# Two projections of the second mixer by high and low parts with two raw weight tiles, and gather slots shared out anew

## The chip, the cores and the metric

The kernel is one program on one core of a Trainium2 chip. The metric is the device time of one execution in microseconds. All data are fp32.

## The reference, cut to what matters

Two transformer blocks run one after the other on 512 tokens of width 1024. Each has a mixer and then a feed-forward layer of experts: every token chooses 16 experts for each of 8 heads, 128 in all, and reads a row `u` and a row `v` of the expert table for each. The second block's mixer is what the change touches.

```python
h = rmsnorm(x, norm1_g)
z = h @ w_in                      # 1024 x 5896, split into nine parts
fq, fk, fv, ff, sq, sk, sv, mq, gl = jnp.split(z, splits, axis=-1)
...                               # three attentions on the parts
gates = jax.nn.sigmoid(gl + b_gate).reshape(B, S, 3, D)
merged = (gates[:, :, 0] * (o_fox @ w_fox_o) + gates[:, :, 1] * (o_swa @ w_swa_o)
          + gates[:, :, 2] * (o_mem @ w_mem_o))
x = x + merged @ w_out
x = x + peer_ffn_2(rmsnorm(x, norm2_g), ...)
# in peer_ffn_2, for each token: e = 128 chosen experts, g = their gates
act = gelu(u[e] @ h) * g
out = act @ v[e]
```

## The kernel before

Activations stand transposed, channels on the partitions and tokens along the row: `xT` and `hT` are 8 chunks of 128 channels by 512 tokens. From the first feed-forward layer on the kernel works on halves of 256 tokens.

**The gather.** The expert layers of both blocks are one stream of 1024 slots: 2 layers x 4 token tiles x 128 chosen experts. A slot reads for each of 128 tokens one row of 2048 fp32 (`u` and `v` side by side, 8 KB) by an indirect DMA that GpSimd issues (`Gather.pool`, L243). VectorE multiplies the `u` half with the token's activation and sums (L309), ScalarE takes the gelu for pairs of slots (L282), VectorE multiplies with the gate (L304), ScalarE makes a diagonal matrix of the weight (L289), and TensorE adds the weighted `v` half into PSUM with four fp32 matmuls (L263). There are 8 row buffers (`BUFS`); the DMA of a slot is issued when the slot 8 before it has been added.

**Beats.** The stream runs inside the other stages. Each stage is a block with one program per engine, and all engines leave it together. A stage is given a range of slots and spreads them evenly over its own steps: after its step i every engine runs its part of the slots of beat i (`Beats.at`). `shared_out` divides a range among the stages of a mixer in proportion to the lengths in `MIXER_LENGTHS`; the ranges are 266 to 508 for the first half of the second mixer and 522 to 764 for the second. `later` holds the slots beside the second tile's choice. A tile's gather can't begin before its choice is finished (`chosen`); what is left runs in `drain_stage`, with nothing beside it.

**The second mixer of one half**, in order: `n3` (norm), `p2` (23 chunks of 128 columns of `w_in_2`: queries, keys, values), `hn` (head norms), `vt` (turning the values), `foxa` (three attentions), `pg` (24 chunks: the gates), `mg2` (merge), `po2` (8 chunks), `n4`, then the query stage `c4` or `c6`, which computes the queries of the experts (16 chunks) and chooses them for its two token tiles. The length named "choose" covers the query chunks and the first tile's choice. The first block's query stage `c2` is the same code; its length "query" is 82 of 266, for 266 slots. Tiles are named by stage, with the half's digit left out: `p2h_ps`, `pgh_w`.

**`project_beside_stage`** (L609), used for `p2` and `pg`, has five weight tiles of 512 KB each (`WEIGHT_TILES`), the first being `first_tile`, loaded in the stage before. SP loads tile n when the product of chunk n - 5 is made. TensorE multiplies the landed fp32 tile with the fp32 activations: 8 products of 128x128 by 256, which the trace shows as 16 matmul instructions (L645). VectorE copies the result from PSUM (L656). ScalarE does nothing but the gather.

**`project_stage`** (L472), used for `p1` (512 tokens) and `poa` (256 tokens) in the first mixer, splits both factors into a high part of type float32r and the remainder: ScalarE copies the raw tile to `whi` (L521), VectorE subtracts to get `wlo` (L565), and the same for the activations once per stage (`hhi` L528, `hlo` L601). TensorE makes three products per 128x128 piece, high by high, high by low, low by high (L546 to L548), 24 matmul instructions per chunk. There are two each of `raw`, `whi` and `wlo`. SP loads raw tile n when `wlo` of n - 2 is made (L510), ScalarE copies when the tile has landed and the product of n - 2 is made. It already has a form that hosts beats (`hosting`), which no call uses.

## Time and profile before

| | us |
|---|---|
| median of 3 runs | 3988.92 (3985.97 to 3993.56) |
| the profiled execution | 3991.26 |
| its span, first to last instruction | 3989.4 |

| engine | busy us | share of the span |
|---|---|---|
| TensorE matmul | 3057.4 | 77% |
| VectorE | 2370.5 | 59% |
| GpSimd | 1152.4 | 29% |
| ScalarE | 915.4 | 23% |

The mean granted clock of TensorE is 0.830 of full speed. The gather's queue moves 1073.81 MB of the 1263.90 MB in all; the gather runs from about 810 us to the end. The second mixer of the first half begins at about 1575 us, that of the second half at about 2465; the last stretch, gather alone, begins at about 3436. Shares of busy time are averages over stages with different limits, so the stretches of single stages are what to read. A matmul's duration in the profile overlaps the next one's; the time that it takes is the distance between two starts.

### The profile page before, as it was taken

How to read it: one execution, taken by the hardware profiler on the slowest of the kernel's cores; microseconds unless marked ns; L12 is line 12 of the kernel's file. 1: busy time of each engine (PE TensorE's matmuls, PEld its weight loads, DVE VectorE, ACT ScalarE, POOL GpSimd, SP SyncE). 2: the span in 40 equal slices, each digit the busy share in tenths (PEclk: the TensorE clock that was granted, in tenths of full speed). 3: DMA queues.
4: the chain of work that ended last, by engine and by line, in shares of the span. 5: the costliest groups of instructions: out<-in, count | busy, mean ns of one | idle time of the engine just before them, and what ended most of it. 6: DMA issues, size and time to landing. Idle time of an engine off the chain costs nothing. (4 is left out here: it accounts for less than half of the span.)

```text
span 3989.4 us, 51160 instructions
## 1 busy us (share of the span) xinstructions
PE 3057.4 (77%) x18686; PEld 1577.7 (40%) x18686; DVE 2370.5 (59%) x6158; ACT 915.4 (23%) x2506; POOL 1152.4 (29%) x1029
## 2 busy tenths in 40 slices
PE   5975596756787765988899865979798876676666
PEld 4853395612354211633455522634465531111111
DVE  6557745476446677457545577457645578655554
ACT  2113232012111112136321111136412111111111
POOL 0000000043333444323323342323333334444442
PEclk8998698867798876977999986969999987766666
DMA  5510002289999999988999997977999999999998
GB/s 214 188 68 1 6 4 93 97 364 400 350 384 372 419 411 393 400 322 309 367 398 373 370 406 269 411 286 264 348 416 376 360 398 395 413 419 417 420 420 354
DMA packets 207064, 1263.90 MB, mean 317 GB/s; under 512 B 25748, under 2 KB 28948, under 8 KB 72356
## 3 DMA queue, kind: packets, MB, share of 16 engines
q0 software_dynamic: 147456, 1073.81, 67.3%
q1 hardware_dynamic: 59368, 186.95, 12.6%
q8 instruction: 143, 2.34, 0.2%
q14 instruction: 97, 0.79, 0.1%
HBM read 1256.17 MB, written 4.46 MB: 316 GB/s over the span
## 5 line engine op out<-in xcount | busy, mean ns | idle before, releaser
L243 POOL DMA_INDIRECT held_z<-in_experts,held_expert x512 | 579.0, 1131 | 1274.6 <-PE held_acc L263 907.6
L263 PE MATMUL held_acc<-held_z,held_diag 64*64 64x512 f32 x4096 | 697.6, 775 | 286.8 <-ACT held_diag L289 262.9
L263 PE MATMUL held_acc<-held_pair,held_diag 64*64 64x512 f32 x4096 | 688.9, 768 | 253.8 <-ACT held_diag L289 248.9
L243 POOL DMA_INDIRECT held_pair<-in_experts,held_expert x512 | 569.6, 1112 | 1047.6 <-PE held_acc L263 971.4
L309 DVE CUSTOM_DVE_ANT_0 held_z<-held_z,held_hrow 128x1024 f32<-128x1024 f32 x512 | 625.5, 1223 | 377.4 <-DMA held_z<-in_experts,held_expert 371.1
L309 DVE CUSTOM_DVE_ANT_0 held_pair<-held_pair,held_hrow 128x1024 f32<-128x1024 f32 x512 | 625.4, 1223 | 369.3 <-DMA held_pair<-in_experts,held_expert 360.7
L289 ACT ACTIVATE held_diag<-held_bands,held_weight 128x64 f32<-128x64 f32 x1024 | 347.7, 340 | 1467.7 <-DVE held_weight L304 1434.3
L263 PEld LDWEIGHTS held_acc<-held_z,held_diag 64*64 64x64 f32 x4096 | 135.2, 157 | 693.3 <-ACT held_diag L289 566.4
L263 PEld LDWEIGHTS held_acc<-held_pair,held_diag 64*64 64x64 f32 x4096 | 134.3, 155 | 670.4 <-ACT held_diag L289 570.8
L282 ACT ACTIVATE held_bent<-held_dot 128x2 f32<-128x2 f32 x512 | 104.0, 203 | 716.1 <-DVE held_dot L309 688.7
L1773 PE MATMUL c_ps<-held_hT,c_w 128*128 128x256 f32 x640 | 151.9, 392 | 0.0
L1250 POOL TENSOR_TENSOR rsolve_decays<-rsolve_ident,rwkv_dend 128x2048 f32<-128x2048 f32 x1 | 3.6, 3612 | 487.2 <-DMA rsolve_ident<-in_id 487.2
L645 PE MATMUL pgh_ps<-held_hT,pgh_w 128*128 128x256 f32 x608 | 141.2, 385 | 3.0 <-DMA pgh_w<-in_w_in 3.0
L1773 PEld LDWEIGHTS c_ps<-held_hT,c_w 128*128 128x128 f32 x640 | 121.8, 195 | 41.1 <-issue 25.1
L645 PE MATMUL p2h_ps<-held_hT,p2h_w 128*128 128x256 f32 x576 | 133.9, 386 | 0.0
L645 PEld LDWEIGHTS pgh_ps<-held_hT,pgh_w 128*128 128x128 f32 x608 | 112.4, 190 | 46.1 <-issue 27.6
L645 PEld LDWEIGHTS p2h_ps<-held_hT,p2h_w 128*128 128x128 f32 x576 | 106.5, 190 | 42.3 <-issue 29.2
L1817 DVE COPY held_z<-c_ps 128x256 f32<-128x256 f32 x64 | 27.2, 425 | 153.2 <-PE c_ps L1773 153.2
L546 PE MATMUL p_ps<-p_hhi,p_whi 128*128 128x512 f32 x272 | 107.9, 397 | 13.2 <-DVE p_wlo L565 13.2
L1773 PE MATMUL c_ps<-held_hT,held_z 128*128 128x256 f32 x384 | 99.0, 416 | 22.9 <-PEq L427 22.9
L547 PE MATMUL p_ps<-p_hlo,p_whi 128*128 128x512 f32 x272 | 106.8, 393 | 0.0
L548 PE MATMUL p_ps<-p_hhi,p_wlo 128*128 128x512 f32 x272 | 106.7, 392 | 0.0
(499 smaller groups left out, 4038.8 us busy)
## 6 DMA issues: line engine op xcount, KB each, us to landing
pgh_w<-in_w_in SPq DMA_DIRECT2D x38, 512.0 KB
p2h_w<-in_w_in SPq DMA_DIRECT2D x36, 512.0 KB
p_raw<-in_w_in SPq DMA_DIRECT2D x34, 512.0 KB, 3.5
p_w_ada<-in_w_ada SPq DMA_DIRECT2D x16, 1024.0 KB, 6.1
c_w<-in_w_query SPq DMA_DIRECT2D x20, 512.0 KB, 3.2
held_z<-in_w_in SPq DMA_DIRECT2D x20, 512.0 KB
c_w<-in_w_peer_q SPq DMA_DIRECT2D x20, 512.0 KB
ada_w<-in_w_ada SPq DMA_DIRECT2D x4, 2048.0 KB, 18.7
```

The lines of the kernel that those rows point to most:

```text
L243: pool.indirect_dma_start(self.pair[m % BUFS], None, self.layers[t // TT][0], bass.IndirectOffsetOnAxis(ap=self.expert[:, t % TT, s:s + 1] ...
L263: last = pe.matmul(self.sum_of(i)[to * BAND:(to + 1) * BAND], diag[band, :], up[band, turn * WIDE:(turn + 1) * WIDE], start=s == 0, stop=s ...
L282: act.activation(self.bent[:, t % 2, at], self.dot[:, t % 2, at], self.layers[t // TT][1]).then_inc(self.bent_made, 1)
L289: act.activation(self.diag[m % DIAGS][:], self.k.bands[:], ACT.Copy, scale=self.weight[:, t % 2, s:s + 1]).then_inc(self.diag_made, 1)
L309: ins = dve.tensor_tensor_reduce(down, down, self.hrow[:, t % TT, :], 1.0, 0.0, ALU.mult, ALU.add, self.dot[:, t % 2, s:s + 1])
L546: pe.matmul(out, hi, hhi[:, c, :], start=c == 0, stop=False)
L547: pe.matmul(out, hi, hlo[:, c, :], start=False, stop=False)
L548: last = pe.matmul(out, lo, hhi[:, c, :], start=False, stop=c == kc - 1)
L645: last = pe.matmul(ps[n % 4][:, 0:tokens], w[n % WEIGHT_TILES][:, c, :], act_in[:, c, :], start=c == 0, stop=c == kc - 1)
L1250: pool.tensor_tensor(decays[:], bcast(ident[:], RP * S // CH, 1), bcast(dend[:], CH, 2), ALU.mult).then_inc(decays_made, 1)
L1773: last = pe.matmul(ps[n % 2][:, 0:tokens], w[n % W][:, c, :], hT[:, c, :], start=c == 0, stop=c == DC - 1)
L1817: dve.tensor_copy(qT[:, n, :], ps[n % 2][:, 0:tokens]).then_inc(used, 1)
```

## The change

`project_stage` gets an argument `first`: with it the first raw tile is the one that the stage before has loaded, and ScalarE waits for that landing. `p2` and `pg` call `project_stage` with beats instead of `project_beside_stage`. So they split weights and activations, make three float32r products instead of an fp32 one, and have two raw tiles of 512 KB instead of five weight tiles. `MIXER_LENGTHS` gets new lengths with the same sum, 253. `mp`, `pob` and `po2` stay with `project_beside_stage`.

```diff
--- before.py
+++ after.py
@@ -469,7 +469,7 @@
                 beats.dve(dve, 1)
 
 
-def project_stage(nc, name, k, w_dram, act_in, kc, chunks, dst, tokens=S, add=None, ada=None, beats=None, normed=None):
+def project_stage(nc, name, k, w_dram, act_in, kc, chunks, dst, tokens=S, add=None, ada=None, beats=None, normed=None, first=None):
 
 
 
@@ -480,7 +480,8 @@
     with ExitStack() as stack:
         r = Room(nc, stack, name)
         hhi, hlo = (r.sb("hhi", [P, kc, tokens], F32R), r.sb("hlo", [P, kc, tokens], F32R))
-        raw, whi, wlo = [[r.sb(f"{n}{u}", [P, kc, P], dt) for u in range(2)] for n, dt in (("raw", F32), ("whi", F32R), ("wlo", F32R))]
+        whi, wlo = [[r.sb(f"{n}{u}", [P, kc, P], F32R) for u in range(2)] for n in ("whi", "wlo")]
+        raw = [first.tile if first and u == 0 else r.sb(f"raw{u}", [P, kc, P]) for u in range(2)]
         ps = [r.ps(f"ps{u}") for u in range(4)]
         scaled, h_hi, h_lo, w_hi, split, made, used = r.sem("scaled", "h_hi", "h_lo", "w_hi", "split", "made", "used")
         w_ready = [r.sem(f"w_ready{u}") for u in range(2)]
@@ -497,7 +498,7 @@
             for n in range(4 * turns, chunks):
                 body(n, n % 4, None)
 
-        with nc.Block() as block:
+        with nc.Block(no_gpsimd_drain=hosting) as block:
             @block.gpsimd
             def _(pool):
                 beats.pool(pool)
@@ -505,6 +506,8 @@
             @block.sync
             def _(sp):
                 def body(n, q, i):
+                    if first and n == 0:
+                        return
                     sp.wait_ge(split, n + 1)
                     src = w_dram[n] if isinstance(n, int) else w_dram[ds(n, 1)].rearrange("a p c e -> (a p) c e")
                     sp.dma_start(raw[q % 2][:], src).then_inc(w_ready[q % 2], 16)
@@ -516,7 +519,10 @@
             @block.scalar
             def _(act):
                 def body(n, q, i):
-                    act.wait_ge(w_ready[q % 2], 8 * n + 16 - 8 * (q % 2))
+                    if first and n == 0:
+                        act.wait_ge(first.landed, 16 * first.count)
+                    else:
+                        act.wait_ge(w_ready[q % 2], 8 * n + 16 - 8 * (q % 2) - (16 if first and q % 2 == 0 else 0))
                     act.wait_ge(made, n + 1)
                     act.activation(whi[q % 2][:], raw[q % 2][:], ACT.Copy).then_inc(w_hi, 1)
 
@@ -2064,7 +2070,7 @@
                fetch=lambda sp: first_tile.fetch(sp, ins["w_in_2"]))
     z, gates = room[:, 0:Y_GATE, :], room[:, 0:3 * DC, :]
     foxT, swaT, memT = hT[:, 0:4, other], hT[:, 4:8, other], room[:, 3 * DC:3 * DC + 4, :]
-    project_beside_stage(nc, own("p2"), ins["w_in_2"], h, DC, Y_GATE, z, HALF, beats["p2"], first_tile)
+    project_stage(nc, own("p2"), k, ins["w_in_2"], h, DC, Y_GATE, z, tokens=HALF, beats=beats["p2"], first=first_tile)
     with ExitStack() as parts:
         a = Room(nc, parts, own("parts"))
         fox_k, swa_k, v = a.sb("fox_k", [P, 4, now.stop]), a.sb("swa_k", [P, now.stop]), a.sb("v", [P, 5, now.stop // P, P])
@@ -2111,7 +2117,7 @@
                             fetch=lambda sp: first_tile.fetch(sp, ins["w_in_2"][Y_GATE:Y_N]),
                             sunk_loads=[(alibi[:], ins["alibi"]), (sinks[:], ins["swa_sinks"].to_broadcast([P, SH]))],
                             loads=kept if half else [], saves=[] if half else [(there, here_) for here_, there in kept])
-    project_beside_stage(nc, own("pg"), ins["w_in_2"][Y_GATE:Y_N], h, DC, 3 * DC, gates, HALF, beats["pg"], first_tile)
+    project_stage(nc, own("pg"), k, ins["w_in_2"][Y_GATE:Y_N], h, DC, 3 * DC, gates, tokens=HALF, beats=beats["pg"], first=first_tile)
     merge_stage(nc, own("mg2"), gates, 0, [(ins["w_fox_o"], foxT), (ins["w_swa_o"], swaT), (ins["w_mem_o"], memT)], h,
                 bias=cols("b_gate_2"), tokens=HALF, beats=beats["mg"],
                 fetch=lambda sp: first_tile.fetch(sp, ins["w_out_2"]))
@@ -2120,8 +2126,7 @@
                fetch=lambda sp: first_tile.fetch(sp, ins["w_peer_q"]))
 
 
-MIXER_LENGTHS = {"n3": 2, "p2": 40, "hn": 15, "vt": 0, "attention": 52, "pg": 42, "mg": 21, "po": 12, "n4": 2,
-                 "choose": 67}
+MIXER_LENGTHS = {"n3": 2, "p2": 28, "hn": 15, "vt": 0, "attention": 58, "pg": 30, "mg": 21, "po": 12, "n4": 2, "choose": 85}
 
 
 FIRST_LENGTHS = {"choose1": 56, "mn": 7, "mp": 14, "mh": 14, "mt": 4, "mg": 15, "po": 13, "n2": 6, "query": 82, "choose": 55}
```

## Rows read from the trace of the kernel before

**Rows 1.** The page, parts 2 and 5: DMA busy tenths in 40 slices; the costliest products.
```profile
DMA  5510002289999999988999997977999999999998
...
L309 DVE CUSTOM_DVE_ANT_0 held_z<-held_z,held_hrow 128x1024 f32<-128x1024 f32 x512 | 625.5, 1223 | 377.4 <-DMA held_z<-in_experts,held_expert 371.1
```

**Rows 2.** Stretches: us, busy by engine (instructions), granted clock, DMA share, GB/s.
```profile
1591.80:1717.00 125.20, 124.04 (x680) 79.46 (x680) 57.18 (x121) 15.37 (x58) 41.27 (x39) 0.98 0.99 397
2479.80:2605.90 126.10, 123.78 (x680) 79.27 (x680) 57.54 (x121) 15.36 (x58) 42.87 (x39) 0.98 0.99 399
1948.70:2078.40 129.70, 128.13 (x708) 82.89 (x712) 62.04 (x140) 16.77 (x62) 39.84 (x38) 0.99 1.01 416
2860.30:2990.00 129.70, 128.09 (x712) 82.66 (x712) 60.35 (x128) 16.77 (x62) 42.24 (x39) 0.99 1.02 417
1630.00:1690.00 60.00, 60.00 (x342) 38.33 (x335) 26.93 (x58) 7.30 (x29) 19.94 (x20) 1.00 1.02 417
3450.00:3900.00 450.00, 311.54 (x1440) 50.87 (x1440) 229.42 (x452) 71.69 (x271) 187.25 (x179) 0.65 1.01 419
```

**Rows 3.** TensorE in order of time, p2 of the first half: start, us, group.
```profile
1591.85 6.32 PE L645 MATMUL p2h_ps<-held_hT,held_z 128*128 128x256 f32 x16 [6.49 <-PEq L427]
...
1661.91 1.04 PE L263 MATMUL held_acc<-held_pair,held_diag 64*64 64x512 f32 x8
1662.88 3.72 PE L645 MATMUL p2h_ps<-held_hT,p2h_w 128*128 128x256 f32 x16
```

**Rows 4.** TensorE in order of time, poa: its first tile, then a later one.
```profile
676.14 0.42 PE L547 MATMUL poa_ps<-poa_hlo,poa_whi 128*128 128x256 f32 x1
676.35 0.41 PE L548 MATMUL poa_ps<-poa_hhi,poa_wlo 128*128 128x256 f32 x1
...
691.30 0.28 PE L546 MATMUL poa_ps<-poa_hhi,poa_whi 128*128 128x256 f32 x1
691.42 0.28 PE L547 MATMUL poa_ps<-poa_hlo,poa_whi 128*128 128x256 f32 x1
```

**Rows 5.** Groups by line, poa, ScalarE and VectorE: count, busy us, mean ns, idle before.
```profile
L521 ACT ACTIVATE poa_whi<-poa_raw 128x1024 fp32r<-128x1024 f32 x8 | 8.5, 1061 | 15.0 <-PE poa_ps L548 11.8 <-DMA poa_raw<-in_w_out 3.3
L528 ACT ACTIVATE poa_hhi<-held_hT 128x256 fp32r<-128x256 f32 x8 | 2.6, 402 | 21.0 <-PEq L1506 21.0
...
L565 DVE TENSOR_TENSOR poa_wlo<-poa_raw,poa_whi 128x1024 fp32r<-128x1024 f32 x8 | 9.8, 1226 | 5.7 <-ACT poa_whi L521 5.7
...
L601 DVE TENSOR_TENSOR poa_hlo<-held_hT,poa_hhi 128x256 fp32r<-128x256 f32 x8 | 2.8, 418 | 1.4 <-ACT poa_hhi L528 1.4
```

**Rows 6.** Weight loads of 512 KB: the page's part 6, and the tile view of mp_w.
```profile
p_raw<-in_w_in SPq DMA_DIRECT2D x34, 512.0 KB, 3.5
...
DMA to landing us min/median/max: 5.2/6.5/7.8
```

**Rows 7.** Waits, p2 of the first half: us in total, times, longest.
```profile
DVE held_z L309 <- DMA held_z<-in_experts,held_expert: 29.5, 18, 2.5
```

**Rows 8.** Stretches of c2, c4, c6, first product to first finished choice.
```profile
1207.00:1431.00 224.00, 166.65 (x956) 78.75 (x959) 148.44 (x446) 37.29 (x129) 90.28 (x80) 0.86 0.99 400
2214.00:2395.00 181.00, 142.08 (x804) 72.52 (x808) 123.20 (x386) 29.43 (x100) 70.31 (x62) 0.90 0.98 395
3123.00:3307.00 184.00, 145.87 (x808) 73.33 (x808) 123.87 (x389) 29.43 (x100) 69.93 (x62) 0.86 0.97 389
```

**Rows 9.** VectorE in order of time: the end of the first choice in c2 and c4.
```profile
1431.06 0.29 DVE L1677 SCALAR_TENSOR_TENSOR held_expert<-c_found 128x128 uint32<-128x128 f32 x1
...
2395.46 0.29 DVE L1677 SCALAR_TENSOR_TENSOR held_expert<-c_found 128x128 uint32<-128x128 f32 x1
```

**Rows 10.** Attention: stretches of both halves, then ScalarE's groups in the first.
```profile
1778.90:1941.50 162.60, 139.53 (x692) 56.31 (x696) 120.16 (x384) 109.61 (x256) 58.38 (x47) 0.81 0.85 318
2674.00:2852.60 178.60, 159.63 (x804) 65.81 (x808) 129.22 (x384) 117.71 (x256) 55.67 (x47) 0.88 0.75 274
...
L952 ACT ACT_TABLE_LOAD x23 | 29.5, 1283 | 5.0 <-PEq L1953 4.6
L282 ACT ACT_TABLE_LOAD x23 | 29.5, 1283 | 0.4
```

## The prediction

> **What bounds the kernel now.** I read the busy digits of the page first, then the table of stretches, then the order of TensorE's work. From slice 8 on the DMA digits stand at 8 to 9 nearly everywhere [rows 1]: this is the expert gather, 1024 slots of 1.049 MB (1073.81 MB of the software queue, read from part 3 of the page, over 1024). The kernel's end is a stretch of gather alone that moves 419 GB/s, 2.5 us a slot [rows 2]. The change doesn't alter how many slots are left for it: both boundaries between which slots are shared out (266 to 508 and 522 to 764) stay. So its whole effect lies inside the two mixers, and since each stage is a block that all engines leave together, stage lengths add up.
>
> The four stretches of the two projections last 125.2, 126.1, 129.7 and 129.7 us [rows 2]. The reader is to see two things. TensorE is busy 124 of 125 and 128 of 130 us: one weight tile is 3.72 us of matmuls and one slot 0.97 us [rows 3], and with 39 slots for 23 tiles, 23 x 3.72 + 39 x 0.97 = 123.4. And at the same time the DMA engines are full: 416 and 417 GB/s in the third and fourth, 417 in the middle of the first [rows 2]. The stages sit on two limits at once. A cheaper product alone gives nothing here; slots have to leave as well, and where they go decides.
>
> **The slots, exactly.** Lengths are shared by whole-number division of 242 slots by 253. Before: p2 39, hn 14, attention 50, pg 40, mg 20, choose 65 (and 14 small ones). After: p2 27, hn 15, attention 55, pg 29, mg 20, choose 82. Each half moves 23 slots out of the projections, 17 into choose, 5 into attention, 1 into hn; po and n4 exchange one.
>
> **TensorE in the new projections.** The stage after the recurrent mixer, poa, is this very code with 256 tokens. Its matmuls start 0.12 us apart at full clock [rows 4], so 24 of them make 2.88 us against 3.72: TensorE's floor is 2.88 + (27/23) x 0.97 = 4.02 us a tile.
>
> **The DMA floor.** A tile is 0.524 MB, and 1.17 slots are 1.23 MB; 1.76 MB at 417 GB/s is 4.2 us a tile.
>
> **The loop through the raw tile, which the change adds.** Before, TensorE reads a landed tile itself and five tiles hide the landing. Now a raw tile is free only when VectorE has subtracted; then SP issues the load, it lands after L, ScalarE copies (1.06 us) and VectorE subtracts (1.23 us) [rows 5], and there are two tiles. With some 0.2 us for the semaphores (an estimate) the period P of a tile obeys 2P = L + 2.5. L is 3.5 us where no gather runs (p_raw), and 5.2 to 7.8, median 6.5, for the same 512 KB beside the gather (mp_w) [rows 6]. That gives P = 3.0 and, beside the gather, 3.9 to 5.2 with 4.5 in the middle. VectorE is in the loop in order, and it also waits there for gather landings as now (29.5 us in the first projection for one half of the buffers) [rows 7], so I take P = 4.6: above the three floors 4.02, 4.2 and 4.5, since loops that lie this close don't overlap perfectly. Ends: 4.2 and 5.2.
>
> Beside this the operations themselves are cheap: per half 47 copies are 50 us of ScalarE and 47 subtractions 58 us of VectorE, but ScalarE is busy 15 of 125 us there and VectorE 57 [rows 2]; with 12 slots fewer at 1.3 us VectorE comes to some 73 of 113. What the waits hold up counts more. Behind ScalarE's wait for a raw tile stand the gather's gelu and its diagonal, for which TensorE waits; behind VectorE's wait for that copy stand the gather's products; and SP issues each load only after the subtraction, where before it had TensorE's word five tiles ahead. The number of loads on SP and the slots' order on GpSimd's queue stay.
>
> **Start of the stage.** TensorE can't begin until eight activations are copied (0.402 each), the last is subtracted, and the first tile is copied and subtracted [rows 5]: 3.2 + 1.06 + 1.23, 5.5 us. Its first tile then runs at the lower level: in poa the matmuls of the first one start 0.21 apart at first [rows 4]; some sixteen of them so (an estimate) make 1.5 us more than 2.88. So 7 us before the regular pace. Before, the first product began at once, at 6.32 us [rows 3], 2.6 over.
>
> **Sum of the projections.** p2: 7 + 23 x 4.6 = 112.8 against 125.2 or 126.1, -12.9 on the mean. pg: 7 + 24 x 4.6 = 117.4, -12.3. At P = 4.2 they are -22 and -22; at 5.2, +1 and +2.
>
> **Seventeen slots more in choose.** The trace holds this experiment already. The third call of the same query stage (c2, first layer) has 82 slots up to its first finished choice, as choose will have; the mixers' have 65. Its stretch lasts 224 us, theirs 181 and 184, at 400, 395 and 389 GB/s [rows 8]; the chosen experts of 1431.06 and 2395.46 mark the ends [rows 9]. So +42 us per half, 2.45 a slot, which is the DMA's price: nothing hides there. Bounds 38 and 45.
>
> By the Trainium skill (DMA: Bandwidth & Descriptors, section Where 436 GB/s comes from) the HBM side limits transfers from HBM into SBUF to about 358 GB/s. By that figure the 17 slots would cost 50 us per half and the sum would end 16 us higher. The trace holds 419 over 450 us [rows 2], and the measurement decides.
>
> **Five slots more in attention, one in hn.** Attention moves 318 and 274 GB/s [rows 10], so DMA time is to be had. But each pair of slots makes ScalarE change tables twice, 23 + 23 loads of 1.283 us in that stage [rows 10], for the gather's gelu between the softmax's exponentials, and TensorE is busy 140 of 163 us. Per slot that is 1.28 us of loads and 0.97 of TensorE: bounds 0 (all in idle time) and 3.2 (the stage's 162.6 us over 50). I take 2.0, near the sum of the two rows: +12 per half for the six. Cover that would have to hold for zero: the 48 us in which ScalarE waits for VectorE.
>
> Forecast per half: -12.9 - 12.3 + 12 + 42 = +29; both halves +58. The profiled execution took 3991.3 us for a span of 3989.4, and the median shown is 3988.9, 2.4 below; against that median it gives 4047 us.
>
> **Rivals.** (A) *The landing is short, and the projections run at the DMA's floor.* With fewer slots the queues are not full; a tile then waits for one slot's transfer at most, L = 3.5 + 2.5 = 6.0, P = 4.25. Projections 104.8 and 109.0: -20.9 and -20.7 per half. With +12 and +42: +12 per half, 4014 us. For it: mp_w's minimum of 5.2. Against: the slots of a saturated queue stand four deep, since SP's load is one of several transfers under way. If attention also takes its slots free, it is 3990. By the Trainium skill (DMA: Bandwidth & Descriptors, section Queues, rings and completion order) a DMA engine serves its queue rows in turn, packet by packet. That is this rival's mechanism, since a tile then waits one turn and never for the whole gather queue; mp_w's median of 6.5 speaks for a little more than one turn.
>
> (B) *The raw loop becomes the bound and is longer than I think.* Landings of 8 us (mp_w's maximum 7.8) and a queued gather operation on ScalarE and VectorE of 1.3 us in each turn give 2P = 11.8, P = 5.9: projections 142.7 and 148.6, +17 and +19; with the rest +90 per half, 4169 us. A half-way case with P = 5.2 gives +57 per half, 4103. For it: three engines and a DMA in one ring, with in-order queues behind each wait. Against: poa runs the ring at TensorE's pace of 2.88 with an idle DMA.
>
> (C) *Faster: the moved slots find idle DMA time.* VectorE's own price of a slot is about 1.3 us (1223 ns and the read of the sum) [rows 1]. If choose were held by VectorE and not by the DMA, 17 slots would cost 22, attention none, and with the projections of rival A the half comes to -20: 3950 us. It decides from a mean price below 41.6/23 = 1.8 us per moved slot. Against it stands the 224 us stretch, with the same 82 slots.
>
> (D) *The change doesn't do what it says:* the product of a tile isn't cheaper, because the clock falls when TensorE idles 16% of these stages instead of 1%. At 0.21 apart it is 5.1 us, P = 6.2 with its slots, +104 per half with the rest and 4197 us. In the stretches of choose TensorE is busy 142 of 181 us at a granted 0.90 [rows 8], so a share of such time is possible, all of it not.
>
> **How the numbers follow.** Forecast (P about 4.6, from 4.4 to 4.9; 4030 to 4080 us): 0.52. A (3989 to 4030): 0.21, of which 0.05 within 0.2%. B with its half-way case (4080 to 4170): 0.17. C: 0.08. D: 0.02. The range leaves out C and the upper part of B: 3990 to 4110. A measurement of this kernel tells 0.2%, 8 us, from no change. Faster: C, 0.08. Same: 0.05 of A and 0.01 between A and C, 0.06. Slower: 0.86.
>
> **What would show it.** Right: p2 and pg at 110 to 120 us, TensorE busy under 90% in them, DMA at 350 to 375 GB/s there where it was 416; choose's first part at 222 to 226 us in both halves; attention 5 to 15 us longer; the last stretch unchanged at 419 GB/s. In the table of waits, ScalarE's copy waiting for the raw tile's DMA is the mark of the loop; if it waits for TensorE instead, A holds. Wrong if choose's first part stays under 210 us, or if the projections fall under 104.

## The result and the profile after

| | before | after |
|---|---|---|
| median, us | 3987.55 | 4068.01 (4059.36 to 4073.63) |
| ratio | | 1.0195, 95% interval 1.0174 to 1.0216 |
| span of the profiled execution, us | 3989.4 | 4057.5 |

The kernel is 80 us slower by the medians, 68 us by the two profiled spans: the profiled execution of the kernel before lies 4 us above its median, that of the kernel after (4059.36) 9 us below its own. Both spans end with the gather alone, 555 us in each; the 68 us lie in the two mixers. Two executions that took far longer at once, one of e2 (14050 us) and one of the kernel before (4707 us), are in the medians below but not in the ratios.

I cut both traces into stages. Each runs from the end of the stage before it to its own last operation. Only hn, mg and po with n4 run on to the next one's first product, and choose runs to the first finished choice. For the kernel after, each row is us, busy time by engine (TensorE, its weight loads, VectorE, ScalarE, GpSimd, with instruction counts), granted clock, DMA share and GB/s. The rows are p2 of both halves, pg of both, choose of both, hn of the first half, attention of both, and a stretch of the gather alone:

```profile
1588.40:1700.10 111.70, 101.03 (x764) 77.06 (x768) 71.99 (x124) 35.93 (x71) 31.85 (x25) 0.93 0.88 339
2515.60:2627.80 112.20, 100.16 (x764) 76.56 (x768) 71.92 (x124) 36.00 (x71) 32.05 (x25) 0.94 0.88 337
1947.60:2076.00 128.40, 109.79 (x828) 82.50 (x824) 79.95 (x149) 39.22 (x81) 35.35 (x32) 0.93 0.91 355
2893.30:3021.60 128.30, 108.62 (x828) 80.45 (x824) 78.16 (x137) 39.20 (x81) 36.44 (x31) 0.95 0.92 358
2208.80:2431.20 222.40, 167.23 (x944) 76.08 (x944) 145.75 (x430) 37.57 (x127) 90.46 (x80) 0.87 1.00 404
3152.40:3377.60 225.20, 170.74 (x944) 77.47 (x944) 145.77 (x429) 37.58 (x127) 93.35 (x80) 0.86 0.99 402
1700.10:1767.20 67.10, 56.23 (x206) 19.77 (x199) 36.00 (x94) 20.06 (x50) 16.20 (x17) 0.62 0.76 265
1767.20:1947.60 180.40, 156.07 (x736) 60.75 (x736) 126.69 (x397) 116.83 (x267) 62.61 (x53) 0.75 0.86 318
2701.40:2893.30 191.90, 171.87 (x856) 69.28 (x856) 135.28 (x397) 125.03 (x267) 62.20 (x53) 0.85 0.77 281
3520.00:3970.00 450.00, 311.53 (x1444) 51.03 (x1448) 228.73 (x452) 71.60 (x270) 186.61 (x180) 0.65 1.01 419
```

The same cut of the kernel before, for p2, pg and hn, where the rows ahead of the prediction began at the first product instead:

```profile
1590.30:1717.30 127.00, 124.04 (x680) 79.46 (x680) 58.65 (x124) 15.37 (x58) 41.58 (x39) 0.97 0.98 393
2478.30:2605.80 127.50, 123.78 (x680) 79.27 (x680) 58.68 (x124) 15.36 (x58) 42.77 (x39) 0.98 0.98 394
1941.50:2078.30 136.80, 129.74 (x724) 83.19 (x720) 64.56 (x145) 17.37 (x65) 43.44 (x42) 0.98 1.01 413
2852.60:2990.00 137.40, 130.48 (x736) 83.27 (x728) 62.89 (x133) 17.38 (x65) 46.64 (x43) 0.99 1.01 414
1717.30:1779.00 61.70, 51.34 (x190) 18.65 (x191) 34.47 (x92) 19.31 (x48) 14.75 (x15) 0.67 0.77 278
```

| stage | before, halves 1 and 2 | after | change, both halves |
|---|---|---|---|
| p2 | 127.0, 127.5 | 111.7, 112.2 | -30.6 |
| pg | 136.8, 137.4 | 128.4, 128.3 | -17.5 |
| hn | 61.7, 68.2 | 67.1, 73.6 | +10.8 |
| attention | 162.5, 178.5 | 180.4, 191.9 | +31.3 |
| choose | 181.5, 183.5 | 222.4, 225.2 | +82.6 |
| all else | | | -8 |

The reader is to see that the projections became cheaper, and that the stages to which their slots went lengthened by more. In p2 TensorE is busy 101 of 112 us where it was 124 of 125 [rows 2], and the DMA engines move 339 GB/s where they moved 397. On the mean of the stage neither limit is reached any more, though in its middle both are near (its row from 1610 to 1690 us stands with e3). In choose they move 404 and 402 GB/s, in a stretch as long as that of c2 [rows 8]. The last row of the first table is the gather alone, 419 GB/s as before [rows 2].

The page's line of the DMA's busy tenths in 40 slices now has 23 slices at 9, where it had 25 [rows 1]:

```profile
DMA  5510002299999998988989996977989999999998
```

How a projection starts, VectorE's rows first and TensorE's below them (start, us, operation):

```profile
1587.88 0.48 DVE L465 SCALAR_TENSOR_TENSOR held_hT<-held_xT,held_columns,n3h_rstd 128x256 f32<-128x256 f32 x1
...
1590.30 2.77 DVE L607 TENSOR_TENSOR p2h_hlo<-held_hT,p2h_hhi 128x256 fp32r<-128x256 f32 x8 [0.80 <-ACT p2h_hhi L534]
1593.39 1.23 DVE L571 TENSOR_TENSOR p2h_wlo<-held_z,p2h_whi 128x1024 fp32r<-128x1024 f32 x1 [0.32 <-ACT p2h_whi L527]
...
1594.72 0.55 PE L552 MATMUL p2h_ps<-p2h_hhi,p2h_whi 128*128 128x256 f32 x1 [11.33 <-DVE p2h_wlo L571]
1595.07 0.42 PE L553 MATMUL p2h_ps<-p2h_hlo,p2h_whi 128*128 128x256 f32 x1
...
1600.11 1.31 PE L263 MATMUL held_acc<-held_pair,held_diag 64*64 64x512 f32 x8
...
1601.58 0.28 PE L553 MATMUL p2h_ps<-p2h_hlo,p2h_whi 128*128 128x256 f32 x1
1601.69 0.28 PE L554 MATMUL p2h_ps<-p2h_hhi,p2h_wlo 128*128 128x256 f32 x1
```

The last operation of the norm ends at 1588.4. The activations' low parts follow the ScalarE copies, the first tile's low part ends at 1594.6, and the first product starts at 1594.72, 6.3 us into the stage. The 24 matmuls of the first tile start 0.21 us apart, the later ones 0.12.

Who waited in the first p2 (us in total, times, longest us):

```profile
DVE p2h_wlo L571 <- ACT p2h_whi L527: 32.8, 18, 3.9
ACT p2h_whi L527 <- DMA p2h_raw<-in_w_in: 23.3, 7, 5.6
...
ACT p2h_whi L527 <- DMA held_z<-in_w_in: 16.9, 7, 4.1
...
ACT p2h_whi L527 <- PE p2h_ps L554: 9.5, 4, 4.0
```

ScalarE's copy waited 23.3 + 16.9 us for landings of the two raw tiles (the first tile is named held_z), and 9.5 us for TensorE. The same two waits are 28.6 and 26.6 us in the first pg.

### The profile page after: what moved, and what is told of

The parts are those of the page before. It is cut to its first block and busy times, and to the rows that moved or that the text cites. A ratio compares the mean times of both kernels' runs of the same rounds, so it can differ in the third digit from the quotient of the medians.

```text
span 4057.5 us, 53054 instructions
## 1 busy us (share of the span) xinstructions
PE 3051.1 (75%) x19438; PEld 1586.2 (39%) x19438; DVE 2486.4 (61%) x6284; ACT 1029.2 (25%) x2640; POOL 1164.3 (29%) x1029
## 5 line engine op out<-in xcount | busy, mean ns | idle before, releaser
L263 PE MATMUL held_acc<-held_z,held_diag 64*64 64x512 f32 x4096 | 721.1, 797 | 313.2 <-ACT held_diag L289 286.2
L263 PE MATMUL held_acc<-held_pair,held_diag 64*64 64x512 f32 x4096 | 701.0, 777 | 265.5 <-ACT held_diag L289 263.6
L243 POOL DMA_INDIRECT held_pair<-in_experts,held_expert x512 | 583.5, 1140 | 999.5 <-PE held_acc L263 930.7
L552 PE MATMUL pgh_ps<-pgh_hhi,pgh_whi 128*128 128x256 f32 x384 | 117.1, 305 | 34.0 <-DVE pgh_wlo L571 33.9
L552 PE MATMUL p2h_ps<-p2h_hhi,p2h_whi 128*128 128x256 f32 x368 | 111.8, 304 | 32.7 <-DVE p2h_wlo L571 32.7
L553 PE MATMUL pgh_ps<-pgh_hlo,pgh_whi 128*128 128x256 f32 x384 | 111.9, 292 | 0.0
L554 PE MATMUL pgh_ps<-pgh_hhi,pgh_wlo 128*128 128x256 f32 x384 | 111.8, 291 | 0.0
L554 PE MATMUL p2h_ps<-p2h_hhi,p2h_wlo 128*128 128x256 f32 x368 | 107.1, 291 | 0.0
L553 PE MATMUL p2h_ps<-p2h_hlo,p2h_whi 128*128 128x256 f32 x368 | 107.0, 291 | 0.0
```

The source lines that it names most:

```text
L243: pool.indirect_dma_start(self.pair[m % BUFS], None, self.layers[t // TT][0], bass.IndirectOffsetOnAxis(ap=self.expert[:, t % TT, s:s + 1] ...
L263: last = pe.matmul(self.sum_of(i)[to * BAND:(to + 1) * BAND], diag[band, :], up[band, turn * WIDE:(turn + 1) * WIDE], start=s == 0, stop=s ...
L552: pe.matmul(out, hi, hhi[:, c, :], start=c == 0, stop=False)
L553: pe.matmul(out, hi, hlo[:, c, :], start=False, stop=False)
L554: last = pe.matmul(out, lo, hhi[:, c, :], start=False, stop=c == kc - 1)
```

## The experiments

Times are medians; ratios are to the kernel before, in runs on the same chip, with their 95% interval. Lengths of stages are from one profiled execution of each kernel.

**The lengths alone** (e1), in the kernel before:

```diff
-MIXER_LENGTHS = {"n3": 2, "p2": 40, "hn": 15, "vt": 0, "attention": 52, "pg": 42, "mg": 21, "po": 12, "n4": 2,
-                 "choose": 67}
+MIXER_LENGTHS = {"n3": 2, "p2": 28, "hn": 15, "vt": 0, "attention": 58, "pg": 30, "mg": 21, "po": 12, "n4": 2, "choose": 85}
```

> The kernel before with the new lengths alone (the old projections keep their five tiles and fp32 products). My theory: the slots that go to choose cost 41 us per half, as in the kernel after, and the old projections shorten only to TensorE's floor, 3.72 + 1.17 x 0.97 = 4.86 us a tile, so by about 12 us each (125 to 114, 130 to 118). With attention and the head norms at +20 per half that is +37 per half, 4060 to 4070 us in all: nearly all of the loss comes from the new lengths, and the new projections are worth only 3 to 8 us per half. Rival: the loss is that of the new projections (their start, their loop through the raw tile); then this kernel stays near 4000 us or below. On attention: if the five more slots cost it 18 and 13 us by themselves, it shows here in the same size; if the lower clock after the new projections made that, attention grows by 10 or less.

Measured: 4055.45 us, 1.0167 (1.0144 to 1.0189). Rows of p2, attention and choose of the first half:

```profile
1587.40:1700.50 113.10, 111.55 (x576) 75.39 (x580) 42.83 (x94) 10.63 (x40) 27.36 (x25) 0.97 0.91 333
1765.60:1934.60 169.00, 144.25 (x736) 57.09 (x736) 126.60 (x397) 116.72 (x267) 61.12 (x53) 0.82 0.89 337
2196.70:2421.70 225.00, 169.82 (x944) 77.09 (x944) 145.73 (x429) 37.56 (x127) 94.84 (x80) 0.87 0.99 401
```

p2 took 113.1 and 113.4 us, pg 129.1 and 129.3, choose 225.0 and 226.1, attention 169.0 and 193.5. So the old projections, with the slots gone, are as short as the new ones within 2 us: in p2 TensorE is busy 111.6 of 113.1 us and stands on its floor. The theory held: the new lengths bring 67 of the 78 us (0.0167 and 0.0195 of 3989). The interval of its ratio overlaps that of the kernel after, so beside these lengths the new projections are worth little in either direction. Attention's +6.5 and +15 against +17.9 and +13.4 in the kernel after left a question for the first half (e9, e11).

**The new projections alone** (e2), the kernel after with the old lengths (the diff above, reversed).

> The kernel after with the old lengths: the new projections with 39 and 40 slots in them. My theory: the DMA's floor (0.524 MB + 1.7 slots of 1.049 MB at 417 GB/s, 5.5 us a tile) holds the stages as before, and the start of 7 us comes on top of it: +6 to +10 us for each of four stages, 4015 to 4030 us, attention and choose as before. Rival: the loop through two raw tiles, in which landings of 7 us and the waits for the gather add up, holds them at 6 us a tile or more, +20 us each, 4070 us and more. A second rival: the products' saving of 0.84 us a tile is worth time even with all slots, 3975 us.

Measured: 4008.15 us, 1.0058 (1.0036 to 1.0080). p2 132.6 and 131.7 us, pg 140.3 and 141.7, attention 160.4 and 174.8, choose 181.7 and 185.0. The first p2:

```profile
1590.20:1722.80 132.60, 111.52 (x864) 77.61 (x864) 87.85 (x154) 40.98 (x89) 48.40 (x39) 0.96 0.94 379
```

TensorE is busy 12 us less than in [rows 2], and the stage is 5.6 us longer; the four stages are +5.6, +4.2, +3.5 and +4.3 us. The trace parts the first into its start and the rest:

```profile
1590.20:1599.00 8.80, 2.47 (x11) 2.50 (x12) 7.54 (x15) 4.91 (x11) 0.00 (x0) 0.50 0.34 122
1599.00:1722.80 123.80, 109.05 (x854) 75.11 (x853) 80.31 (x141) 36.07 (x78) 48.40 (x39) 1.00 0.98 398
```

After the start the DMA moves 398 GB/s, as it did before the change (397 [rows 2]), so with all slots in it the DMA holds the stage, and the start comes on top. Little is loaded during the start (122 GB/s). The four stages lost somewhat less than the 6 to 10 us I had put; in this one what follows the start is a little shorter, 123.8 us, where the kernel before took 125.2 from its first product [rows 2].

**A third raw tile** (e3), in the kernel after. The excerpt shows the tiles and SP's wait; ScalarE's wait and the tile that ScalarE and VectorE read follow suit:

```diff
+        R = 3 if first else 2
-        raw = [first.tile if first and u == 0 else r.sb(f"raw{u}", [P, kc, P]) for u in range(2)]
+        raw = [first.tile if first and u == 0 else r.sb(f"raw{u}", [P, kc, P]) for u in range(R)]
...
-                    sp.wait_ge(split, n + 1)
+                    if not first:
+                        sp.wait_ge(split, n + 1)
+                    elif n >= R:
+                        sp.wait_ge(split, n - R + 3)
```

> The kernel after with a third raw tile in the two projections, so that a load has one tile's time more to land; nothing else is changed (a fourth does not fit into SBUF). My theory: the loop through the raw tile sets part of the pace of 4.5 us a tile; with three it goes to the floor of the DMA, 4.2 us, 5 to 8 us per stage, 20 to 30 us in all, 4040 to 4050 us, and the waits of ScalarE's copy for the raw tile (40 and 55 us in the two stages of the first half) fall under 10. Rival: the pace is that of the DMA or of VectorE's order; then the time stays within 5 us of the kernel after and the waits only move.

Measured: 4024.98 us, 1.0110 (1.0077 to 1.0142): 43 us below the kernel after by the medians and 34 by the ratios (0.0085 of 3989), more than the 20 to 30 expected. p2 104.2 and 104.0 us, pg 117.1 and 116.7. The first p2 and its waits:

```profile
1591.20:1695.40 104.20, 97.84 (x760) 75.02 (x764) 73.70 (x125) 36.30 (x71) 42.76 (x25) 0.95 0.91 357
```

```profile
ACT p2h_whi L534 <- PE p2h_ps L561: 40.4, 20, 3.6
...
DVE p2h_wlo L578 <- ACT p2h_whi L534: 13.3, 20, 0.7
```

In p2 no wait for a raw tile's landing is left, and ScalarE's copy waits for TensorE, 40.4 us; in the first pg 6.1 us of such waits are left of 55. TensorE is busy 97.8 of 104.2 us. The middle of the stage, from 1610 to 1690 us, in the kernel after and then in e3:

```profile
1610.00:1690.00 80.00, 77.35 (x599) 58.20 (x597) 50.58 (x85) 24.69 (x48) 25.57 (x21) 0.98 0.97 383
1610.00:1690.00 80.00, 80.00 (x633) 60.40 (x632) 57.10 (x94) 27.80 (x52) 37.88 (x22) 1.00 1.00 400
```

With the third tile TensorE has no gap left there, and the DMA engines are full too (busy share 1.00, 400 GB/s); the stage's mean of 357 GB/s is low because of the start. So the new projections then stand on two limits at once, as the old ones did. The load of a raw tile also takes longer than in mp_w [rows 6]; the tile view of p2h_raw in e3 has

```profile
DMA to landing us min/median/max: 3.3/8.0/9.2
```

and e2 has 3.2, 7.9 and 9.9. Going from two raw tiles to three took 7.6 and 8.2 us off p2 and 11.3 and 11.6 off pg, 39 us in all: that is what the loop had cost.

**Ten slots from attention to choose** (e4), in the kernel before:

```diff
-MIXER_LENGTHS = {"n3": 2, "p2": 40, "hn": 15, "vt": 0, "attention": 52, "pg": 42, "mg": 21, "po": 12, "n4": 2,
-                 "choose": 67}
+MIXER_LENGTHS = {"n3": 2, "p2": 40, "hn": 15, "vt": 0, "attention": 42, "pg": 42, "mg": 21, "po": 12, "n4": 2,
+                 "choose": 77}
```

> The kernel before with the attention's length 42 and choose 77 in place of 52 and 67: 10 slots per half go from attention to choose. In the kernel after a slot more in attention cost 2.7 to 3.6 us and one in choose 2.4. If these prices hold in both directions, this kernel is faster by 10 x (3.2 - 2.4) per half, 10 to 20 us in all, 3970 to 3980 us. Rival: attention's price is high only above 50 slots, or came from the clock; taking slots away returns 1 to 2 us each, and this kernel is 8 to 28 us slower, 3996 to 4016 us.

Measured: 3998.78 us, 1.0039 (1.0024 to 1.0054), slower. The first attention:

```profile
1773.30:1910.00 136.70, 117.18 (x616) 50.48 (x620) 108.70 (x362) 95.38 (x233) 48.71 (x38) 0.89 0.85 309
```

Attention fell by 25.8 us in the first half and by 13.6 in the second, for ten slots fewer by the lengths; choose grew by 28.3 and 27.0 for nine more. So a slot gives back 2.6 us in the first attention and 1.4 in the second, and costs 3.0 to 3.1 in choose. My price of attention (3.2) was too high, by less than a fifth in the first half and by more than half in the second, and that of choose (2.4) too low. The rival was right on the sign and on the second half (1 to 2 us a slot), not on the first.

**Without the gelu** (e7, e8). Both leave out the gelu of the two expert layers, with a copy in its place, so that ScalarE needs no other table for the gather; e7 is the kernel before, e8 is e1 with this edit:

```diff
-    layers = [(ins["experts1"], ACT.Gelu_apprx_tanh, mod[:, 5 * DC:6 * DC]), (ins["experts2"], ACT.Gelu, None)]
+    layers = [(ins["experts1"], ACT.Copy, mod[:, 5 * DC:6 * DC]), (ins["experts2"], ACT.Copy, None)]
```

> The kernel before with the gelu of both expert layers left out (a copy stands in its place), so that ScalarE needs no change of tables for the gather; the instructions are otherwise the same. It serves as the base of the next kernel. My theory: the 46 loads of 1.283 us are 59 us of ScalarE's 110 busy us in the attention, and ScalarE is on the attention's path; without them the two attentions of 162.5 and 178.5 us lose 20 to 40 us each, until the DMA (318 GB/s) or TensorE (140 us busy) holds them, 3910 to 3950 us in all. Rival: TensorE holds the attention; then they lose under 8 us each.

> The kernel before with the new lengths and the gelu of both expert layers left out. My theory: with the table loads gone a slot more in attention costs what the DMA or TensorE asks, 1 to 2.5 us, so attention is 5 to 13 us longer than in the one with the old lengths, and of the 6.5 and 15 us that the new lengths cost it with the gelu, the loads' part (2 more pairs, 5 us) is gone; choose still costs 41 to 43 us more. Rival: the loads play no part in a slot's price; then attention grows by the same 6.5 and 15 us.

Measured: e7 3980.07 us, 0.9973 (0.9956 to 0.9991); e8 4032.76 us, 1.0111 (1.0075 to 1.0147). The first attention of e7, then of e8:

```profile
1781.50:1926.70 145.20, 123.25 (x696) 51.02 (x696) 119.73 (x384) 50.82 (x211) 55.84 (x48) 0.93 0.96 358
```

```profile
1766.90:1925.90 159.00, 137.88 (x736) 55.55 (x736) 125.94 (x397) 52.21 (x218) 64.02 (x53) 0.85 0.94 358
```

ScalarE's busy time falls from 110 [rows 10] to 51 us, the 59 us of loads, and attention to 145.2 and 174.6 us: -17 in one half, -4 in the other. The rival holds for the second half; in the first my 20 to 40 was nearly reached, but the clock rose at the same time, 0.93 against 0.81, and TensorE was busy 16 us less. The profiled execution of e7 was also 10 us faster than e7's median (3969.87 against 3980.07), so the 17 us may be on the high side. The price of the slots is what counts here: with the new lengths attention grows by 13.8 and 5.9 us without the loads, 19.7 together, and by 6.5 and 15.0 with them, 21.5 together. Half by half the two differ, in opposite directions; in the sum of both halves hardly. So the table loads are not what makes a slot dear in attention. I had leaned on them in the prediction. Choose grew by 39.2 and 36.8 us between the two, a little less than the 41 to 43 expected.

**More slots beside the second tile's choice of the first half** (e5, e6), in the kernel before; that piece has 14 slots and 279 GB/s:

```diff
-    starts = [half_done, first_layer_done]
+    starts = [half_done, first_layer_done + 16]
```

and + 28 in e6.

> The kernel before with 16 more slots beside the second tile's choice of the first half (30 in place of 14) and 16 fewer in the second half's mixer. There the DMA moves 279 GB/s and VectorE is full at 97%. My theory: a slot there costs VectorE's 1.3 us and up to 1.8 (32 more slots make the same piece 58 us longer in the second half), while one in the second mixer costs 2.5 in choose, 2.5 in the projections, 1.5 in attention: -8 to -16 us, 3973 to 3981 us. Rival: the second mixer's slots come back for 1 us each, since TensorE's floor stands right under; then it is even or slower, 3988 to 3996 us.

> The same with 28 more slots beside the second tile's choice (42) and 28 fewer in the second half's mixer. My theory: the price there rises to the DMA's 2.5 us a slot as the DMA fills (42 slots in 68 us of choice would be 620 GB/s, so the stage must grow to about 105 us), so this gains no more than the kernel with 16: within 5 us of it. Rival: the gain is in proportion, 28/16 of it.

Measured: e5 3990.68 us, 1.0007 (0.9992 to 1.0021); e6 3995.00 us, 1.0020 (1.0003 to 1.0037). The piece in the kernel before and in e5:

```profile
2395.50:2463.90 68.40, 36.70 (x172) 12.35 (x168) 64.09 (x274) 11.45 (x30) 19.13 (x18) 0.67 0.75 279
```

```profile
2388.80:2480.10 91.30, 53.76 (x296) 14.73 (x296) 82.02 (x312) 17.88 (x54) 33.90 (x33) 0.73 0.93 355
```

It grew by 22.9 us for 15 slots, 1.5 each, within the price I had put (1.3 to 1.8). But the second mixer gave back only 6.0 in p2, 6.0 in attention, 1.9 in pg and 7.7 in choose for its 16 slots, some 1.4 each: the kernel came out even, as the rival had it, at a price between its 1 us and mine. In p2 TensorE was then busy 120.0 of 121.5 us. With e6 the piece took 109.9 us at 402 GB/s, 1.6 a slot, near the 105 I had put (where my 620 GB/s should read 648). In the second choose the five slots of e5 gave back 7.7 us, 1.5 each, and the three more of e6 nothing (175.9 and 176.5 us). So the price of 2.4 to 3.1 us a slot holds for slots added to choose as it was in the kernel before, and not for slots taken out of it. No better kernel came of either.

**Attention back at its old length** (e9), and the kernel after again (e11):

```diff
-"attention": 58, "pg": 30, "mg": 21, "po": 12, "n4": 2, "choose": 85}
+"attention": 52, "pg": 30, "mg": 21, "po": 12, "n4": 2, "choose": 91}
```

> The kernel after with the attention's length back at 52 and choose at 91: the new projections with 27 and 29 slots, the attention with its old slots. In the kernel after the first half's attention took 180.4 us with TensorE at the lower level for 89 us of it; with old projections and the same slots 169.0 us and 61 us low; with new projections and the old slots 160.4 us and 57 low. Theory: it is the five slots more that bring the low time, so attention comes back to 160 to 164 us and 172 to 180 in the second half; six slots more in choose cost 15 us per half. In all 4055 to 4070 us. Rival: the shorter new projection before it brings it; attention stays at 172 us or more, and the kernel takes 4080 us.

> The kernel after once more, unchanged, for a second profile. If the low time of TensorE in the first half's attention (89 of 180.4 us) belongs to this program, it comes again within some us, and attention takes 178 to 183 us; if it was chance, attention takes about 169 us as with the old projections and the same slots, and the low time is near 61 us.

Measured: e9 4046.33 us, 1.0150 (1.0122 to 1.0178); e11 4065.79 us, 1.0198 (1.0169 to 1.0227). The first attention of e9, then of e11:

```profile
1771.30:1927.20 155.90, 136.99 (x688) 55.37 (x688) 119.02 (x382) 106.29 (x252) 57.41 (x47) 0.81 0.89 326
```

```profile
1770.60:1952.20 181.60, 156.22 (x736) 60.80 (x736) 126.89 (x397) 116.86 (x267) 64.10 (x54) 0.75 0.87 318
```

TensorE runs at 2.4 GHz or at half of it, so a granted share of c over T us means 2(1 - c)T us at the lower level (to 2 us or so, since c has two digits). That is 90 us in the kernel after (0.75 of 180.4) and 91 in e11 (0.75 of 181.6), so it belongs to the program. The first attention of e3, which has three raw tiles and the lengths of the kernel after, shows it a third time:

```profile
1761.20:1941.40 180.20, 156.08 (x736) 60.80 (x736) 126.71 (x397) 116.87 (x267) 62.28 (x53) 0.75 0.87 318
```

In e9 it is 59 (0.81 of 155.9), in e1 61 (0.82 of 169.0), in the kernel before 62 (0.81 of 162.6) [rows 10]. The slots are needed for it, as e9 shows: attention comes back to 155.9 us, a little under the 160 expected; e2, with new projections and old slots, has 58 us of it. But e1, with the same slots and old projections, doesn't have it. Both together make 29 us more at 1.2 GHz and 11 us more attention than e1. Why the pair does it stays open. It does it in the first half only: the second attention took 191.9, 190.9 and 192.1 us in the kernel after, e11 and e3, and 193.5 in e1.

e9 is also 19 us faster than the kernel after (1.0150 against 1.0198 in the same comparison), and below the 4055 to 4070 that I had put: six slots fewer returned 24.5 and 21.8 us in attention and cost 10.7 and 8.2 in choose.

**Three raw tiles and lengths between the two** (e10):

```diff
-MIXER_LENGTHS = {"n3": 2, "p2": 28, "hn": 15, "vt": 0, "attention": 58, "pg": 30, "mg": 21, "po": 12, "n4": 2, "choose": 85}
+MIXER_LENGTHS = {"n3": 2, "p2": 34, "hn": 15, "vt": 0, "attention": 52, "pg": 36, "mg": 21, "po": 12, "n4": 2, "choose": 79}
```

on top of e3.

> The kernel with three raw tiles and lengths between the two: p2 34, pg 36, attention 52, choose 79. By the DMA's floor (0.524 MB and 1.43 slots at 417 GB/s, 4.86 us a tile) and 7 us of start p2 takes 119 and pg 124 us; the attention is as before; choose has 11 or 12 slots more at 2.5 us. Sum per half -8 - 13 + 29 = +8, 4000 to 4010 us: once the DMA holds both places, a slot moved between them gives nothing, and the start of the new projections is what is left. Rival: the cheaper product is worth its 0.84 us a tile where the loop is gone; then 3970 us.

Measured: 4010.87 us, 1.0066 (1.0043 to 1.0090), just above the theory's 4000 to 4010 and far from the rival's 3970. The first p2:

```profile
1590.80:1707.80 117.00, 106.42 (x816) 78.51 (x816) 79.52 (x140) 38.14 (x80) 40.84 (x32) 0.94 0.93 374
```

p2 took 117.0 and 116.0, pg 127.3 and 126.1, choose 212.1 and 213.0, attention 158.5 and 180.0, near the kernel before. Six slots more than in e3 made p2 12.4 us longer on the mean, 2.1 each, and six fewer took 14.5 and 13.6 us off choose, 2.3 each: with the raw tile's loop out of the way a slot costs about the same in both places, and moving it gains next to nothing. Against the kernel before, p2 and pg are 9.5 to 11.5 us shorter each and choose 30 us longer. That the start of the new projections is what is left over fits e2, but no run takes the start away. No kernel that computes the whole came out faster than the one before; the nearest, e5, is level with it.

## Why the prediction was right, step by step

Forecast 4047 us, slower, within 3990 to 4110; measured 4068. The causes and their order were right. The forecast change was +58 us, the measured one +80 by the medians and +68 by the two profiles; the 12 us between these two lie in which executions were profiled, and no stage accounts for them. Against the 68 us, attention and hn were forecast 18 us too low over both halves, and the other stages gave back 8 us that I hadn't forecast and that hid part of it.

*The projections.* Forecast -12.9 for p2 and -12.3 for pg per half; measured -15.3 and -8.8 on the mean. The sum per half is right within 1.2 us. The start came as worked out (6.3 us to the first product, the exchange of the blocks included, against 5.5, and a whole first tile at 0.21 us a matmul, 2.2 over a later one). The pace came out at 4.5 us a tile in p2, (111.7 - 6.3 - 2.2)/23, and by the same steps at 4.8 in pg, where the first product starts 10.9 us after attention's end (the trace of TensorE has it at 1958.5), against my 4.6. My split between the two was off for that reason: I had let pg start as early as p2. The mark that I had named stands in the waits, 40.2 us of ScalarE's copy for the raw tiles. Counted from ScalarE, the copies start 4.7 to 4.8 us apart in all four stages, and each starts 6.5 to 7.6 us after SP issued its load (the medians of the four stages, 7.1 on the mean). Copy, subtraction and the next issue follow one another within 0.03 us nearly always; the 0.2 us that I had put for the semaphores came from no row. So 2P = 7.1 + 1.06 + 1.23 + 0.06, and P is 4.7: the equation of the loop held, with a landing somewhat longer than my 6.5 and steps somewhat closer. e3 shows that the loop was the bound: with a third tile the pace is (104.2 - 8.5)/23 = 4.2. I had called that value the DMA's floor; in e3 TensorE's floor of 4.0 and the DMA's of 4.2 are reached together in the middle of the stage.

*Seventeen slots in choose.* Forecast +42 per half; measured +40.9 and +41.7, in e1 +43.5 and +42.6. This was the largest term, and the best founded: c2 had done it already [rows 8]. The stretch of 222.4 us was inside my 222 to 226, the second at 225.2 too. By the Trainium skill (DMA: Bandwidth & Descriptors, section Where 436 GB/s comes from) some 358 GB/s per core, a stack's 716 GB/s over its two cores, would be the limit. The kernel after, one core at work, holds 419 over 450 us and 404 over choose, so here the trace disagrees with it.

*Five slots in attention and one in hn.* This is the term that was mis-sized. Forecast +12 per half, at 2.0 us a slot within bounds of 0 and 3.2; measured +23.3 and +18.8. Six slots at 3.9 and 3.1 us: the first is above my upper bound. I had taken the price from the table loads (1.28) and TensorE's 0.97. e7 and e8 show that the loads have next to no part in it: 19.7 us for the slots without them, 21.5 with them. What I had left out is TensorE's clock. In hn it is 0.67 of full speed and in the first attention 0.81, and at the lower level TensorE is busy nearly all the time there. From 1760 to 1800 us, across the end of hn, in the kernel before and after:

```profile
1760.00:1800.00 40.00, 37.48 (x128) 14.74 (x127) 22.75 (x60) 14.06 (x32) 8.30 (x10) 0.54 0.83 320
1760.00:1800.00 40.00, 37.97 (x129) 15.46 (x131) 21.35 (x64) 15.97 (x36) 8.29 (x9) 0.50 0.85 329
```

So a slot costs TensorE up to twice 0.97 us there (an estimate from these rows and [rows 3]), and more low time slows all of its matmuls, attention's own too. In the first half the runs part the two. At a like clock (kernel before and e1, 62 and 61 us low) the five slots cost 6.5 us, 1.3 each, within my bounds. The other 11.4 us came in the kernel after, with 29 us more at the lower level. In hn the low time rose as well, from 41 to 51 us. In the second attention the clock explains less. Here are e10 and e11, at the same 0.88:

```profile
2670.70:2850.70 180.00, 161.10 (x816) 66.07 (x816) 129.29 (x384) 117.78 (x256) 55.80 (x48) 0.88 0.77 273
2706.80:2897.70 190.90, 168.21 (x856) 67.72 (x856) 135.40 (x397) 124.92 (x267) 60.66 (x53) 0.88 0.79 286
```

Five slots more cost 10.9 us, 2.2 each, and 2.7 each in the kernel after. What a slot there waits for stays open. The upper bound, a stage's length over its slots, was no bound: the slots can lengthen the rest of the stage, and more low time came with them.

*What the rest gave.* The other stages together gave 8 us back. Half of it is po with n4, 2 us shorter in each half. The rest is differences of 1 to 2 us in several stages, which one profile of each kernel can't part from chance.

*The marks.* Of those that I had named, choose, the last stretch, the length of p2 and ScalarE's wait came as put. pg (128.4) lay outside my 110 to 120, which I had given for both by counting from the first product; TensorE was busy 85 to 90% of these stages, where I had put under 90; the DMA moved 337 to 339 GB/s in p2, under my 350, and 355 to 358 in pg; attention grew by 17.9 us in the first half, over my 15.

*The rivals.* A (the DMA's floor, 4014 us) fell: it needed landings that ScalarE's copy doesn't wait for. Its landing of 6.0 us was the bare 3.5 and one slot's 2.5; in the kernel after the copy starts 6.5 to 7.6 us after the issue. The Trainium skill (DMA: Bandwidth & Descriptors, section Queues, rings and completion order) says that queues are served in turn. If one slot's transfer is one turn, the trace agrees in part only: the tile waits for somewhat more than one. B (the loop at 5.2 or more) had the right mechanism and came out too large; its landing of 8 us is what e2 and e3 have, where the DMA is fuller. C fell by choose, and by e4: the moved slots cost 3.0 us there, above the 1.8 from which it would decide. D: TensorE stayed at a granted 0.93 to 0.95 in the projections, so the products were cheaper as worked out.

What my sum had not asked is what the change would bring by its parts. e1 answers: the old projections free the same time as the new ones when the slots go, because TensorE's own floor, 3.72 + 1.17 x 0.97 = 4.86 us a tile without a start, is as good as 4.6 with one. The cheaper product is paid for by its own start (e2) and by the raw tile's loop (e3).

## What to carry to other kernels

Where a stage stands on two limits at once, TensorE and the DMA, making one cheaper gives nothing until load leaves the other, and the load must go where that other resource is idle; price it at the receiving place, best from a stage of the same code that already carries the larger load. When a tile must pass through two more engines before it is free, count landing, copy and subtraction against the number of tiles, and take the landing from where the DMA is as full as it will be: here two tiles were one too few. An idle share of the DMA in a stage is no free room: attention moved 318 GB/s, and slots still cost 1.3 to 3.6 us each in it.

## What the runs showed of the hardware

Loads of another table in ScalarE, 59 us of its 110 busy us in the first attention, were worth 17 us there and 4 in the second when they were gone, 9 us in the whole kernel by the medians, 11 by the ratio of 0.9973: an engine can be half filled with them at small cost.

The first half's attention with the same slots ran with TensorE at 1.2 GHz for 61 us (e1) or for 90 us (kernel after, e11, e3), according to which projection stood in the kernel; the second half's showed no such difference. In the old projection TensorE had been busy 111.6 of 113.1 us at a granted 0.97, in the new one 101.0 of 111.7 at 0.93; hn, 65 and 67 us long, lies between it and the attention.

The same plain 512 KB load from HBM takes 3.5 us with no gather [rows 6], a median of 6.5 beside it in mp_w [rows 6], and of 8.0 in e3, where the DMA engines are full. An indirect load of one slot, 1.05 MB, lands about 10 us after its issue in that stage, about four times the 2.5 us that one slot's bytes take, so some four are under way at once.
